# A second unit three rows behind the first, high parts first, and table matmuls in a norm's waits

## What is computed

```python
for l in range(DEPTH):                       # DEPTH = 2
    mod = cond @ ada_w[l] + ada_b[l]         # shift, scale, gate for each of three sub-layers
    h = _modulate(_rmsnorm(x, ffn1_norm_g[l]), sh1, sc1)
    x = x + 0.5 * g1 * _swiglu(h, ffn1_w_in[l], ffn1_w_out[l])
    h = _modulate(_rmsnorm(x, mix_norm_g[l]), sh2, sc2)
    x = x + g2 * _token_mixing(h, ...)
    h = _modulate(_rmsnorm(x, ffn2_norm_g[l]), sh3, sc3)
    x = x + 0.5 * g3 * _swiglu(h, ffn2_w_in[l], ffn2_w_out[l])
return _rmsnorm(x, final_norm_g)
```

## Time and profile before

| | before |
|---|---|
| median of 3 runs | 2489.05 us (2486.96 to 2492.75) |
| profiled execution, its own time | 2490.49 us |
| its span | 2488.8 us |
| mean granted clock of TensorE | 0.985 of full speed |
| PE busy | 2381.6 us (96%), 13428 matmul passes |
| DVE busy | 1268.2 us (51%) |
| ACT busy | 871.3 us (35%) |
| chain that ended last | PE 90%, DVE 5%, ACT 3% |

### The profile page before, as it was taken

How to read it: one execution, slowest core, us unless ns; L and a number is a source line. 1 busy time by engine, 2 the same in 40 slices (tenths; PEclk the granted TensorE clock), 3 DMA queues, 4 the chain that set the end, 5 groups by cost and what they waited for, 6 DMA issues and landing times.

```text
span 2488.8 us, 35088 instructions
## 1 busy us (share of the span) xinstructions
PE 2381.6 (96%) x13428; PEld 1926.2 (77%) x13428; DVE 1268.2 (51%) x1659; ACT 871.3 (35%) x1232; POOL 93.3 (4%) x165
## 2 busy tenths in 40 slices
PE   3999999999999999999989999999999999999998
PEld 3888887777767778888878888877776777788887
DVE  6554555554365654433355545565446565444333
ACT  3431233332355444223344222334224553432222
POOL 2100010000000000000001001000000000000000
PEclk9999998999999999999999999999999999999999
DMA  7564562222213424432235645522222342343231
GB/s 279 193 212 151 186 209 89 84 76 79 89 64 123 157 93 146 158 103 101 99 103 194 204 150 194 195 76 68 78 86 73 102 157 101 118 156 130 85 110 59
DMA packets 93063, 319.27 MB, mean 128 GB/s; under 512 B 11856, under 2 KB 12240, under 8 KB 92832
## 3 DMA queue, kind: packets, MB, share of 16 engines
q1 hardware_dynamic: 57888, 215.87, 25.6%
q0 software_dynamic: 21248, 76.79, 9.4%
q10 hardware_dynamic: 13824, 25.17, 2.9%
HBM read 303.11 MB, written 14.68 MB: 128 GB/s over the span
## 4 chain that ended last, share of the span: by engine, by line
PE 90%; DVE 5%; ACT 3%; issue 1%; DMA 1%; SPq 0%; ACTq 0%; DVEq 0%
PE PS L417 76%; PE PS L857 3%; PE PS L429 3%; PE PS L626 3%; DVE wl L1215 1%; DVE ada L1670 1%; ACT wh L910 1%; ACT sco L1102 1%; DMA ada<-in_ada_w_dram 0%; PE PS L527 0%; PE PS L789 0%; PE PS L634 0%; PE PS L801 0%; PE PS L833 0%; PE PS L746 0%
## 5 line engine op out<-in xcount | busy, mean ns | idle before, releaser
L1215 DVE TENSOR_TENSOR wl<-raw,wh 128x1024 fp32r<-128x1024 f32 (+2 forms) x360 | 466.2, 1295 | 808.6 <-ACT wh L910 808.5
L417 PE MATMUL PS<-uh,wh 128*128 128x512 f32 x2144 | 857.2, 400 | 16.2 <-DVE wl L1215 11.0
L417 PE MATMUL PS<-ul,wh 128*128 128x512 f32 x2144 | 837.7, 391 | 0.0
L417 PE MATMUL PS<-uh,wl 128*128 128x512 f32 x2144 | 837.5, 391 | 0.0
L910 ACT ACTIVATE wh<-raw 128x1024 fp32r<-128x1024 f32 (+2 forms) x360 | 401.5, 1116 | 917.9 <-PE PS L417 887.4
L417 PEld LDWEIGHTS PS<-uh,wh 128*128 128x128 f32 x2144 | 403.7, 188 | 117.0 <-issue 19.8
L417 PEld LDWEIGHTS PS<-uh,wl 128*128 128x128 f32 x2144 | 404.0, 188 | 86.1
L417 PEld LDWEIGHTS PS<-ul,wh 128*128 128x128 f32 x2144 | 404.1, 188 | 84.1 <-issue 4.3
L417 PE MATMUL PS<-hh,wh 128*128 128x512 f32 x704 | 273.9, 389 | 0.0
L417 PE MATMUL PS<-hl,wh 128*128 128x512 f32 x704 | 273.9, 389 | 0.0
L417 PE MATMUL PS<-hh,wl 128*128 128x512 f32 x704 | 273.9, 389 | 0.0
(11 more groups left out here) (230 smaller groups left out, 1834.4 us busy)
## 6 DMA issues: line engine op xcount, KB each, us to landing
raw<-in_ffn_in_dram SPq DMA_DIRECT2D x176, 512.0 KB, 3.5
ada_raw<-in_ada_w_dram POOLq DMA_DIRECT2D x144, 512.0 KB, 3.8
raw<-in_mix_in_dram SPq DMA_DIRECT2D x88, 512.0 KB, 3.4
raw<-in_ffn_out_dram SPq DMA_DIRECT2D x32, 768.0 KB, 4.4
raw<-in_ffn_out_dram SPq DMA_DIRECT2D x32, 640.0 KB, 3.9
g_in<-gates_dram ACTq DMA_DIRECT2D x48, 256.0 KB, 3.1
ada<-in_ada_w_dram SPq DMA_DIRECT2D x16, 512.0 KB, 11.0
raw<-in_mix_up_dram SPq DMA_DIRECT2D x16, 512.0 KB, 3.6
```

What stands on the lines that cost most here:

```text
L417: mm = e.matmul(PS[:, bank, :], w[:, j % 2, k * P:(k + 1) * P], v[:, k, :], start=(k == 0 and w is wh and v is xh), stop=(k == K - 1 and w ...
L1215: TTo(wl[:, j % 2, 0:K * P], raw[:, j, 0:K * P], wh[:, j % 2, 0:K * P], ALU.subtract)\
```

## The change

`first_pair` is given another order. Its loop has KD + 3 steps; in step i the first unit does row i and the second unit row i - 3. Each unit's three matmuls of a row are now high by high, low weights by high data, high weights by low data, so that the two that need only `uh` come first. The waits are finer: the first unit waits for `uh` of its row, then ahead of its third matmul for `ul`; the second unit waits for its own `wl` (`lo_ready`) only at its row 0, and for nothing else.

`keep_busy` is new: full-float matmuls of `ident` by 256 columns of the table `cos` into bank 3, which is read by nobody then. Four go behind the matmuls of `ssq`, three behind those of `sq`, eight behind the broadcast; none in norm (0,0), and in the last norm only the four and the three. PE waits once, in norm (0,1), for the tables' load.

```diff
+LAG = 3
...
-            def first_pair(l, n, banks, there):
-
-                e.wait_ge(lo_ready.sem, n + (2 + RAW))
-                for k in range(KD):
-                    there(k)
-                    for j in range(2):
-                        for w, v in ((wh, uh), (wh, ul), (wl, uh)):
+            def first_pair(l, n, banks, s):
+
+
+
+                for step in range(KD + LAG):
+                    for j, k in ((0, step), (1, step - LAG)):
+                        if not 0 <= k < KD:
+                            continue
+                        if k == 0:
+                            e.wait_ge(lo_ready.sem, n + (j + 1 + RAW))
+                        if j == 0:
+                            e.wait_ge(uh_done.sem, uh_done.at(l, 8 * s + k + 1))
+                        for w, v in ((wh, uh), (wl, uh), (wh, ul)):
+                            if j == 0 and v is ul:
+                                e.wait_ge(ul_done.sem, ul_done.at(l, 8 * s + k + 1))
                             mm = e.matmul(PS[:, banks[j], :], w[:, j, k * P:(k + 1) * P], v[:, k, :],
-                                          start=(k == 0 and w is wh and v is uh), stop=(k == KD - 1 and w is wl))
+                                          start=(k == 0 and w is wh and v is uh), stop=(k == KD - 1 and v is ul))
                         if k == KD - 1:
                             mm.then_inc(unit_done.sem, 1)
...
+            def keep_busy(l, s, count):
+
+
+                if (l, s) == (0, 0):
+                    return
+                for _ in range(count):
+                    e.matmul(PS[:, 3, 0:256], ident[:, :], cos[:, 0:256], start=True, stop=True)
+
             def norm(l, s):
 
+                if (l, s) == (0, 1):
+                    e.wait_ge(tables_in.sem, 16 * 11)
 
                 e.wait_ge(ssq_done.sem, ssq_done.at(l, 6 * (s + 1)))
...
+                keep_busy(l, s, 4)
                 e.wait_ge(sq_done.sem, sq_done.at(l, 8 * (s + 1)))
...
                 mm.then_inc(norm_mm.sem, 1)
+                keep_busy(l, s, 3)
                 e.wait_ge(rstd_done.sem, rstd_done.at(l, s + 1))
...
                 mm.then_inc(rstd_mm.sem, 1)
+                if l < DEPTH:
+                    keep_busy(l, s, 8)
...
-                        first_pair(l, l * UNITS + n0, (0, 2),
-                                   lambda k: e.wait_ge(ul_done.sem, ul_done.at(l, 8 * s + k + 1)))
+                        first_pair(l, l * UNITS + n0, (0, 2), s)
...
-                first_pair(l, l * UNITS + MIX, (0, 1), lambda k: e.wait_ge(ul_done.sem, ul_done.at(l, 8 + k + 1)))
+                first_pair(l, l * UNITS + MIX, (0, 1), 1)
```

## The result

| | before | after |
|---|---|---|
| median | 2490.41 us (2486.96 to 2492.75, 4 runs) | 2472.18 us (2471.7 to 2472.9, 4 runs) |
| ratio | | 0.9931, 95% interval 0.9919 to 0.9944 |
| span of the profiled execution | 2488.8 us | 2470.4 us |
| mean granted clock | 0.985 | 0.998 |

The change is faster by 0.69%, some 17 to 18 us; 2475.6 was forecast, a gain of 13.4 us, with 2471 to 2484 as the range. In a later session the changed kernel had a median of 2472.46 us over 5 runs against 2490.74 for the kernel before.

What follows compares the result with a forecast made beforehand. TensorE bounds the kernel, so time is won only where it idles or runs at half clock, at the norms. Gains 4.2 + 1.3 + 1.4 + 2.4 + 2.3 + 2.4 - 0.6 = 13.4 us from 2489.05 gave 2475.6 us, range 2471 to 2484.

Steps and rivals of the forecast that it cites:

- The third unit's wait goes: Behind each norm's first pair: the 1.82 to 1.88 us wait for `wl` vanishes, 0 to 0.3 us left.
- chain of 2.94: From the first unit's last matmul through ACT's split and DVE's subtraction to the third unit's start: 2.94 us.
- Row 3 gates the pair: In the first pair, `ul` row 3 sets the end; 37 matmuls, 8.4 us, follow without waiting; third unit at D + 14.8.
- D: Start of DVE's first scaling in a norm, forecast 6.07 us behind the first sums where it was 5.47.
- Tables: Filler matmuls in the norms: four take 1.72 us, three 1.3, eight 3.45; the broadcast starts 1.5 us late in all.
- The clock stays up: Granted clock at 1.00 from first sums to third unit in five norms; forecast chance 0.80.
- rival 1: In the norms the clock falls once and returns under the tables, giving back all 13.4 us: 2489; chance 0.08.
- rival 2: In the norms table matmuls do not count as work for the clock, which stays low: 2513 us; chance 0.05.
- Rival 3: Behind the first pair the third unit still waits 1 us at six norms: 2481.5 us; chance 0.07.
- Norm (1,0): D stays where it was: DVE splits two units first there, so D stays at 6.47 us behind the first sums; gain 2.3 us.
- Norm (0,0) gains 2.4: Norm without tables, starting at half clock: end at D + 15.1 for D + 17.7, gain 2.4 us.
- The mixers and FFN stretches change only by the 1.6 us behind norm (0,1): Outside the norms, only 8 matmuls at half clock behind norm (0,1)'s third unit's wait were priced, 1.6 us.

Runs made afterwards that it cites:

- experiment 2: The kernel before with the table matmuls added and the old order of the first pair kept: 2487.39 us, ratio 0.9990.
- experiment 3: The changed kernel with a lag of 2 rows for 3, tables kept: 2472.24 us, ratio 0.9935.
- experiment 5: The changed kernel with no tables and a lag of 0 rows, leaving high data first and the finer waits: 2484.90 us, ratio 0.9984.
- experiment 4: The kernel before, unchanged, run again for a second profile: 2489.29 us, ratio 1.0003.
- experiment 9: The changed kernel with 1, 1 and 4 tables per norm for 4, 3 and 8, plus three and two in each mixer's gaps: 2464.86 us, ratio 0.9900.
- experiment 1: The changed kernel with no table matmuls, the lag and its order kept: 2470.35 us, ratio 0.9923.

## Why the prediction was right, and where it was off

- *The third unit's wait goes, because 12 matmuls cover a chain of 2.94.* Right. No wait is left with 3 rows; 0.52 us with 2; all of it with none and with the tables alone (experiments 2, 3, 5).
- *Row 3 gates the pair at D + 14.8.* Right: D + 14.9 (the sum's own terms, 6.46 + 37 x 0.227, give 14.86), with the wait at row 3 seen at 0.34 us for 0.5. The gate moved as worked out with 4 rows (D + 15.55) and with 12 tables (20.9 + 0.88).
- *Tables: 0.43 us each, loads hidden, first sums to broadcast 4.9, D at 6.07, third unit at 20.9.* Right: 0.43, 4.81, 5.99 and 20.90. The rule of the Trainium skill ("TensorE: Matmul & The Clock Gate", Part 3, "The mechanism"), that a weight load overlaps a running matmul only in another row group, does not fit these rows either: 8 passes with their loads of 0.19 took 1.97 us. The same section of the Trainium skill also lets a load into a background weight buffer go ahead of running matmuls, and that would fit them.
- *The clock stays up.* Right, at 1.00 in the five norms; rivals 1 and 2 fell, and the clock held through passes of a plain full-float multiply by the identity. Rival 3 fell too: the split starts at once.
- *Norm (1,0): D stays where it was.* Wrong by 0.65 us. The split of two units was taken as the fixed bound of D, but DVE starts it only behind the reciprocal, which the seven tables made late:

```profile
1248.23 0.18 DVE L1253 RECIPROCAL rstd_tok<-root_tok 128x4 f32<-128x4 f32 x1 [2.74 <-ACT root_tok L951]
1249.11 2.36 DVE L1237 TENSOR_TENSOR wl<-raw,wh 128x1024 fp32r<-128x1024 f32 x2 [0.70 <-ACT wh L932]
1251.38 1.40 DVE L1274 SCALAR_TENSOR_TENSOR t_buf<-x,scale_eff,PS 128x512 f32<-128x512 f32 x2
```

  The reciprocal comes at 3.97 us behind the first sums for 3.32 before, and D at 7.12 for 6.47. A bound that is itself released by the delayed step moves with it.
- *Norm (0,0) gains 2.4.* Right: 2.8.
- *The mixers and FFN stretches change only by the 1.6 us behind norm (0,1).* This is the mis-sized term, and the whole difference between 13.4 and 18 us. Half clock behind the third unit's wait was priced once, for the one place where the first profile had it. The second profile of before and that of experiment 5 have it twice, that of experiment 2 three times: over these profiles it stood behind five of the six waits, at 1.6 us each, and no profile without the wait has it there. The mixers were priced at nothing. 3.2 us of theirs is chance in the first profile (experiment 4), from a longer wait for the low part of a merged row (2.41 us for 1.0) and a half-clock stretch behind it. The remaining 2.5 us between the second profiles are one half-clock stretch each instead of two and a shift of these waits. Whether the change has a hand in that count is open: the two profiles of the changed kernel and that with 2 rows have one in each mixer; those with 12 tables, with the lag alone, with the tables alone and with the order alone have two in each; those with 4 rows and with the small tables one and two. That the result still lies in the range, at its low end, is in part luck: the gain beyond 13.4 us was allowed there for tables that cost the sums nothing, and they cost what the forecast said.
- *What the prediction didn't ask* is what each half of the change gives. It added lag and clock into one length of 20.9. Taken apart, the lag with its order gives all of it, 19 us, and the tables, beside it, cost 2.2 us in the six norms (132.4 us together for 130.2) and some 0.5 in the last, of which the medians show 1.8, between two sessions. With all gaps filled in both, they cost 3.9. At half clock the lone rows of the first unit mostly still finish before DVE's row 3. What half clock does cost is the slower broadcast, 0.3 us of D, and up to 0.7 us where it lasts longer: against experiment 9, the five norms of experiment 1 are 2.1 us longer in all. No run has the lag with the old order within a row, so what the order adds to the lag is open.

## What to carry to other kernels

When two products share a start and the buffer of the first gates the next, stagger them by as much work as the refill chain lasts, no more: the lone rows at the start are bounded by the producer, and a fourth one cost 0.63 us here (its gate comes 1.32 us later, with 0.68 us less work behind it). Before filling waits to hold the clock, look whether anything in the stretch is bound by PE; fill only up to the gap, counted from when the filler may begin. And price half clock at every wait it can follow, not only at the one where a single profile shows it.

## What the runs showed of the hardware

- A gap of 1.8 to 2.7 us in PE's work was followed by about 3.4 us at 1.2 GHz at some executions and not at others, at the same place of the same kernel (behind norm (0,1) in one profile of before, behind (0,0) and (0,2) in the other). Each cost about 1.6 us: an FFN stretch with one took 349.88 us for 348.28. The runs of the kernel before spread over 5 us, those of the kernel with every gap fitted over less than 1 us (4 runs); that fits, though no single run was traced twice.
- In some profiles such a stretch also began behind a shorter gap with little work about it: the mixer's 1.37 us between sums of 16 columns and 64x64 matmuls (at 502.5 with the lag alone, not in the changed kernel). With that gap filled there was none (experiment 9).
- Full-float passes of 256 columns with weights of 128x128 ran 0.215 us apart, their loads of 0.19 us hidden, and the clock stayed at 2.4 GHz through them in five norms of the changed kernel.
